# Second wide layer as seven block products for eight, with its down projection a phase behind

## The reference

```python
up = causal_depthwise_conv_2(x @ w_up[l], conv_ffn[l])      # w_up: 1024 x 5632, 3 taps in time
a_ff, b_ff = jnp.split(up, 2, axis=-1)                      # 2816 gate and 2816 value columns
x = layer_norm_2(DEEPNORM_ALPHA * x + (jax.nn.silu(a_ff) * b_ff) @ w_down[l], ln2_g[l], ln2_b[l])
```

## Time and profile before

| what | value |
|---|---|
| median of 3 runs | 3225.45 us (3222.04 to 3225.76) |
| profiled execution, its own time | 3221.95 us |
| span of the profiled execution | 3220.2 us |
| mean granted TensorE clock | 0.962 of full |
| second wide layer, first up product to end | 2453.5 to 3220.2 us |
| PE busy in the whole span | 2994.7 us (93%) |

### The profile page before, as it was taken

The page is one execution under the profiler, slowest core; times in us unless marked ns, Lnnn a source line. Parts: engine busy times, 40 slices in busy tenths (PEclk is TensorE's granted clock), DMA queues, the critical chain, the costliest instruction groups (busy, mean ns, idle before and its releaser), DMA issues.

```text
span 3220.2 us, 35921 instructions
## 1 busy us (share of the span) xinstructions
PE 2994.7 (93%) x15137; PEld 2466.7 (77%) x15137; DVE 1542.0 (48%) x2205; ACT 915.1 (28%) x1250; POOL 784.2 (24%) x482
## 2 busy tenths in 40 slices
PE   8979976689999999999999899799999999999997
PEld 7767766567788788888878899666677888888885
DVE  4775657756644365565244344211135333343335
ACT  3211255422443311112265122211112223222231
POOL 0343401013233322123121454101212211121113
PEclk9989987789999999999999999899999999999999
DMA  4121231122333532212011100211121111111112
GB/s 141 55 60 62 71 97 56 60 98 79 105 113 110 191 114 88 105 66 97 19 53 40 47 21 14 80 58 33 40 92 40 53 40 53 40 52 53 40 53 78
DMA packets 183360, 222.40 MB, mean 69 GB/s; under 512 B 8528, under 2 KB 146448, under 8 KB 181152
## 3 DMA queue, kind: packets, MB, share of 16 engines
q1 hardware_dynamic: 174528, 208.46, 20.0%
q10 hardware_dynamic: 8672, 11.65, 1.0%
HBM read 179.02 MB, written 41.07 MB: 68 GB/s over the span
## 4 chain that ended last, share of the span: by engine, by line
PE 79%; DVE 11%; POOL 3%; ACT 3%; DMA 2%; issue 2%; SPq 0%; ACTq 0%; POOLq 0%; DVEq 0%
PE bank L127 77%; DVE f L158 5%; POOL f L158 3%; DVE f L166 2%; PE bank L142 2%; DVE f L175 1%; DVE r L158 1%; ACT f L147 1%; ACT f L150 1%; DMA f<-gr_s 1%; ACT r L150 1%; DVE f L163 1%; DMA f<-x 0%; DMA f<-w_in 0%; SPq L195 0%
## 5 line engine op out<-in xcount | busy, mean ns | idle before, releaser
L127 PE MATMUL bank<-r,r 128*128 128x512 f32 (+5 forms) x11412 | 2404.0, 372 | 42.6 <-DVE r L158 21.1
L127 PEld LDWEIGHTS bank<-r,r 128*128 128x128 f32 (+1 forms) x11412 | 1984.3, 190 | 452.9 <-issue 44.9
L158 POOL TENSOR_TENSOR f<-f 128x512 f32<-128x512 f32 (+5 forms) x249 | 363.1, 1465 | 1365.1 <-DVE f L166 445.0
L158 DVE TENSOR_TENSOR f<-f,bank 128x512 f32<-128x512 f32 (+2 forms) x564 | 349.6, 641 | 581.1 <-PE bank L127 506.4
L150 ACT ACTIVATE r<-f 128x2048 fp32r<-128x2048 f32 (+4 forms) x188 | 298.7, 1616 | 610.0 <-DMA f<-a_s 248.9
L150 ACT ACTIVATE f<-bank 128x512 f32<-128x512 f32 (+5 forms) x393 | 202.0, 520 | 663.8 <-PE bank L127 600.3
L158 POOL TENSOR_TENSOR r<-f,r 128x2048 fp32r<-128x2048 f32 (+1 forms) x48 | 220.3, 4590 | 623.0 <-ACT r L150 623.0
L127 PE MATMUL bank<-f 128*128 128x128 f32 (+8 forms) x2296 | 326.2, 308 | 43.1 <-ACT f L150 14.4
L158 DVE TENSOR_TENSOR r<-f,r 128x2048 fp32r<-128x2048 f32 (+4 forms) x140 | 258.9, 1860 | 208.1 <-ACT r L150 206.5
L166 DVE SCALAR_TENSOR_TENSOR f<-f,f 128x1024 f32<-128x1024 f32 (+3 forms) x167 | 194.9, 1175 | 306.5 <-ACT f L147 277.4
L127 PEld LDWEIGHTS bank<-f 128*128 128x128 f32 (+2 forms) x2296 | 280.3, 204 | 75.0 <-issue 19.3
(11 more groups left out here) (32 smaller groups left out, 553.4 us busy)
## 6 DMA issues: line engine op xcount, KB each, us to landing
f<-w_in SPq DMA_DIRECT2D x31, 1024.0 KB, 5.5
f<-w_up SPq DMA_DIRECT2D x44, 512.0 KB, 5.1
f<-w_mlp_in SPq DMA_DIRECT2D x64, 256.0 KB, 3.2
a_s<-f SPq DMA_DIRECT2D x64, 256.0 KB, 2.1
f<-w_mlp_out SPq DMA_DIRECT2D x16, 1024.0 KB, 4.9
f<-a_s SPq DMA_DIRECT2D x16, 1024.0 KB, 7.0
f<-w_down SPq DMA_DIRECT2D x11, 1024.0 KB, 4.9
f<-w_out SPq DMA_DIRECT2D x8, 1024.0 KB, 5.2
```

Source lines behind the costliest of these rows:

```text
L127: return self.g.matmul(out, lhs, rhs, start=start, stop=stop, skip_group_check=True)
L158: return self.g.tensor_tensor(out, a, b, op)
```

## The change

The second wide layer gets the scheme of the first. Block 0 is still made by four full products (`U.first`). Blocks 1 to 21 are each made by P1 to P7. ACT's prefix copies and DVE's additions write straight into `raw`. The taps of a block's gate tile (`tap(n, 0)`) come at the end of its turn, those of its value tile (`tap(n - 1, 1)`) in the next turn, after the first addition. The product of gate and value (POOL) goes to DRAM, H is moved out to DRAM and back, and the down projection runs after all blocks, as in the first wide layer. The code of the first layer moves into shared classes without a change of its order. The core of the difference:

```diff
 def pe_f(k, g):
-    for j in range(22):
-        for n, (e, h) in enumerate(S.order(j)):
...
-            g.sum3(b, [((vs[0][:, x, :], vs[1][:, x, :]), (xh[:, x, hs], xl[:, x, hs])) for x in range(8)]).then_inc(
-                *k.up("up products", "f", "up", j, e, h))
-        if j % 2 and 1 < j < 21:
-            i = j // 2 - 1
-            pe_down(k, g, "f", [(i, S.down[i])], S.panels, S.acts)
-    pe_down(k, g, "f", [(i, S.down[i]) for i in (9, 10)], S.panels, S.acts, 4)
+    for n, (e, h) in enumerate(S.order()):
+        if n == 2:
+            pe_flush(k, g, "o2", k.g.H)
+        U.first(g, S.first, "o2", e, h)
+    U.begin(g, 1)
+    for n in range(1, 22):
+        x = k.bank("f", "x", n)
+        U.side(g, n, "z", [2, 3], 2, True)
+        y = U.side(g, n, "y", [4, 5], 5, False)
+        g.wait_ge(*k.past("f", "s1", n))
+        U.product(g, n, 6, x, False, False)
+        g.wait_ge(*k.past("f", "s5", n))
+        U.product(g, n, 3, y, False, True)
+        g.wait_ge(*k.past("f", "s2", n))
+        U.product(g, n, 7, x, False, False)
+        if n < 21:
+            U.begin(g, n + 1)
+        g.wait_ge(*k.past("f", "c22", n))
+        U.product(g, n, 4, x, False, True)
+    D.products(g)
+    for c in range(NC):
+        D.last_products(g, c)

 def act_f(k, g):
+    for n in range(1, 22):
+        if n > 1:
+            c21(n - 1)
+        tap(n - 1, 1)
+        if n < 21:
+            U.round(g, n + 1, 0)
+        else:
+            D.round(g, 0, "d")
+        prefix("s5", n, 1, 1, 5, "y")
+        if n < 21:
+            U.round(g, n + 1, 1)
+        else:
+            D.round(g, 0, "a")
+        prefix("s2", n, 0, 1, 6, "x")
+        tap(n, 0)
+        if n < 21:
+            prefix("s1", n + 1, 0, 0, 1, "x")
+        if n == 1:
+            silu(0)
+        silu(n)

 def dve_f(k, g):
+    U.low_t(g, S.t2, S.kept)
+    taps(0, 0)
+    for n in range(1, 22):
+        add(n, 0, 0, "s1", 2, "z").then_inc(*k.drain("relu low", "f", "z", n))
+        taps(n - 1, 1)
+        if n < 21:
+            U.sums(g, n + 1)
+            U.rest(g, n + 1, 0)
+        else:
+            D.weight_low(g, 0)
+        add(n, 0, 1, "s2", 3, "y").then_inc(*k.drain("relu low", "f", "y", n))
+        if n < 21:
+            U.rest(g, n + 1, 1)
+        add(n, 1, 1, "s5", 7, "x").then_inc(*k.up("relu low", "f", "c22", n))
+        taps(n, 0)

 def pool_f(k, g):
+    U.t4(g, "o2", S.kept, S.t2)
+    for n in range(22):
+        g.wait_ge(*k.past("f", "silu", n))
+        g.wait_ge(*k.past("f", "tap", n, 1, 0))
+        g.tt(S.acc[n % 2], S.acc[n % 2], S.gate, MUL).then_inc(*k.up("squares", "f", "gated", n))
+        if n == 20:
+            D.acts_low(g, 0)

 def sp_f(k, g):
+    sp_away(k, g, "f", "o2", H, 0)
...
+    for n in range(1, 22):
...
+            g.wait_ge(*k.past("f", "P", n - 1, 4))
+            if n < 21:
+                U.load(g, n + 1, "A22")
+            else:
+                down(0)
+        g.wait_ge(*k.past("f", "P", n, 5))
+        if n + 2 < 22:
+            U.load(g, n + 2, "A11", "A12", "A21")
...
+        store(n - 1)
```

More of the change, by code:

```diff
@@ L2148, in pe_flush, with operand_rows @@
         pe_turn(k, g, tag, H[:, c, :], c)
[L2153 to L2206, removed]
+def operand_rows(k, hi, lo):
+    return tuple(v[:, at:at + 2048].rearrange("p (k t) -> p k t", k=4) for v, at in ((k.rb, hi), (k.rb, lo), (k.sb, lo)))
 class Seven:
@@ L2444, in sp_m @@
             g.wait_ge(*k.past("m", "P", 15, 6))
[L2445 to L2448, removed]
+            sp_back(k, g, "m", H)
         store(n, 1)
@@ L2468, in pe_m @@
 def pe_m(k, g):
-    S, U = k.m, k.m.seven
+    S, U, D = k.m, k.m.seven, k.m.down
     a_done(k, g)
@@ L2760, in dve_m @@
             U.rest(g, n + 1, 1)
[L2762 to L2780 removed]
+    D.adds(g, k.H)
     for c in range(NC):
@@ L2783, in dve_m @@
             S.gating.rest(g, 0, 0)
-        add(15, 13, c)
-        g.wait_ge(*k.past("drain", "m", "down", 15, c, 1))
+        D.last_adds(g, k.H, c)
         dve_ln(k, g, "m", c, k.H[:, c, :])
@@ L3804, in o2_done, with order, made @@
+        self.gate = k.sb[:, Y + 7168:Y + 7168 + NT]
+        self.lnw = k.sb[:, Y:Y + 2048]
+        homes = [((ring, X), (ring + 2048, X + 2048)), ((M, M + 2048), (M + 4096, M + 6144)), ((W, W + 2048), (W + 4096, W + 6144))]
+        self.down = Down(k, "f", k.A["w_down_2"], homes, 11)
+    def order(self):
+        return [(e, h) for h in range(2) for e in range(2)]
+    def made(self, n, e, h):
+        return ("drain", "f", "first", e, h) if n == 0 else ("f", f"c{e + 1}{h + 1}", n)
 def o2_done(k, g):
@@ L3879, in act_f, with tap @@
-    S.panels.round(g, S.down[10] + 1)
+    def tap(n, e):
+        for h in range(2):
+            g.wait_ge(*k.past(*S.made(n, e, h)))
+        if e:
+            if n:
+                g.wait_ge(*k.past("f", "gated", n - 1))
+        elif n >= 2:
+            g.wait_ge(*k.past("f", "stored", n - 2))
+        cw = P["conv_ffn"][:, 3 * (n + 22 * e):3 * (n + 22 * e) + 3]
+        o = S.gate if e else S.acc[n % 2]
+        g.act(o, S.raw[n % 2][e][:, 2:2 + NT], ACT.Identity, scale=cw[:, 2:3]).then_inc(*k.up("relu", "f", "tap", n, e, 2))
@@ new lines, in silu, with first @@
+    def silu(n):
+        o = S.acc[n % 2]
+        g.wait_ge(*k.past("f", "tap", n, 0, 0))
+        g.act(o, o, ACT.Silu).then_inc(*k.up("relu", "f", "silu", n))
+    def first(u):
+        e, h = S.order()[u]
+        g.wait_ge(*k.past("f", "first", e, h))
+        g.cp(S.raw[0][e][:, half_slice(h, 2)], k.bank("f", "first", e, h)).then_inc(*k.drain("relu", "f", "first", e, h))
+    first(0)
+    first(1)
+    act_block(k, g, U, "o2", S.kept, 6)
+    act_block(k, g, U, "o2", S.kept, 7)
+    U.high_t1(g, "o2")
@@ new lines, in act_f, with copy, prefix, c21 @@
+    U.round(g, 1, 0)
+    first(2)
+    U.high_t2(g, S.t2)
+    U.round(g, 1, 1)
+    first(3)
+    tap(0, 0)
+    U.high_t34(g)
+    def copy(name, n, e, h, p, bank):
+        if n >= 2:
+            g.wait_ge(*k.past("f", "tap", n - 2, e, 0))
+        g.wait_ge(*k.past("f", "P", n, p))
+        return g.cp(S.raw[n % 2][e][:, half_slice(h, 2)], k.bank("f", bank, n))
+    def prefix(name, n, e, h, p, bank):
+        copy(name, n, e, h, p, bank).then_inc(*k.up("relu", "f", name, n))
+    def c21(n):
+        copy("c21", n, 1, 0, 4, "x").then_inc(*k.drain("relu", "f", "x", n))
+        k.also("f", "c21", n)
@@ L3908, in dve_f, with taps, add @@
-    S.panels.rest(g, S.down[10] + 1, 0)
-    dve_down(k, g, "f", 10, k.g.H, 8, lambda c: dve_ln(k, g, "f", c, k.g.H[:, c, :], S.lnw))
+    def taps(n, e):
+        cw = P["conv_ffn"][:, 3 * (n + 22 * e):3 * (n + 22 * e) + 3]
+        o = S.gate if e else S.acc[n % 2]
+        for d in (1, 0):
+            g.wait_ge(*k.past("f", "tap", n, e, d + 1))
+            g.stt(o, S.raw[n % 2][e][:, d:d + NT], cw[:, d:d + 1], o, MUL, ADD).then_inc(*k.up("relu low", "f", "tap", n, e, d))
+    def add(n, e, h, s, p, bank):
+        o = S.raw[n % 2][e][:, half_slice(h, 2)]
+        g.wait_ge(*k.past("f", s, n))
+        g.wait_ge(*k.past("f", "P", n, p))
+        return g.tt(o, o, k.bank("f", bank, n), ADD)
@@ L3912, in pool_f @@
+    taps(21, 1)
+    D.adds(g, k.g.H)
+    for c in range(NC):
+        D.last_adds(g, k.g.H, c)
+        dve_ln(k, g, "f", c, k.g.H[:, c, :], S.lnw)
 def pool_f(k, g):
-    S = k.f
+    S, U, D = k.f, k.f.seven, k.f.down
     o2_done(k, g)
```

576 lines of the change are left out of this document (290 added, 286 removed).

## The result

The changed kernel takes 3253.43 us (median of 4 runs, 3249.55 to 3254.47) against 3223.74 us of the kernel before on the same chip (4 runs, 3219.76 to 3225.76): ratio 1.0091, 95% interval 1.0074 to 1.0109. It is slower by some 29.7 us. The time is in the prediction's whole range (3210 to 3262), but outside the range of its likeliest case (3224 to 3250), which had 3236. The course is that of the rival "a fall behind every wait", which gave 3257. (A fall is a stretch at the lower of TensorE's two clock levels.)

What follows compares the result with a forecast made beforehand. PE was taken to bound the second layer: 66.9 us saved, waits of 2.80 per block eating 53.2; with all legs, entry and tail +1.1, plus +10 for clock falls, giving 3236 us on the median, range 3210 to 3262.

Steps and rivals of the forecast that it cites:

- likeliest case: Whole kernel: PE waits 2.80 us per block and a third of the waits bring a clock fall; 3236 us, chance 0.47.
- a fall behind every wait: Rival, second layer's turns: each wait before P7 is followed by the lower clock, +1 + 30, 3257 us, chance 0.13.
- The saving: Second wide layer on PE: 288 matmuls fewer ahead of 3167.64, worth 66.9 us at 232.2 ns each.
- The start: Second layer, from the start to block 1's P7: 54.2 us, including 1.6 for a lower clock.
- The wait in each turn: Before P7, blocks 2 to 20: path 10.86 against 8.06, so PE waits 2.80 us, released by ACT's copy s2.
- the bare four: DVE's four weight sums with no POOL instruction among them: 2.42 us.
- The third rival: POOL does not get between DVE's sums: they take 2.4, PE waits 0.4 per block; 3181 us, chance 0.14.
- The turn, the down projection and its drain: After block 20: last turn and transition 28.5, nine down pairs 200.6, then 24 matmuls and drain 5.8 us.
- Entry and end: Before the second layer's first product +1.0 us from extra copies; at the tail +1.5 us from chunk 1's later products.
- I take a third: Clock falls behind the 19 waits: between none and all (30 us), a third assumed, +10 us.
- clock 0.5 shows up in most turns: Sign that the forecast is wrong: the lower clock level in most turns; none would also count against it.
- lower bound of 3210: Low end of the whole range 3210 to 3262, given as 3227 less twice its error, leaving out the third rival.

Runs made afterwards that it cites:

- the filled kernel: Changed kernel plus eight matmuls that nobody reads ahead of TensorE's wait on s2 in each of 20 turns: 3222.87 us, ratio 1.0.
- the first experiment: Changed kernel with VectorE's four sums of the next block put before the value taps: 3166.49 us, ratio 0.9825.
- The second experiment: Changed kernel with taps still ahead of the sums, but POOL's gating product waiting for the sums to end: 3183.0 us, ratio 0.9882.
- the fourth: Changed kernel with the value taps moved even earlier, ahead of the addition for c11: 3205.13 us, ratio 0.9942.
- the fifth: Changed kernel plus a second, unread POOL product of 128x512 ahead of the gating product in 19 blocks: 3282.97 us, ratio 1.0176.
- the kernel with the eighth product back: Changed kernel in the order of the first experiment, plus 12 unread matmuls in each of 21 turns ahead of the wait on c22: 3218.34 us, ratio 0.9984.

## Why the prediction came out as it did

- **The saving**, 66.9 us at 232.2 ns a matmul: right. Where nothing waits the pace holds over 1560 matmuls (231.3 ns each) and over 1908 (232.3). The 131 ns of the Trainium skill ("TensorE: Matmul & The Clock Gate", Back-to-back issue gap) does not hold for this kernel's matmuls; no stretch came near it.
- **The start**, 54.2: measured 53.2 (2450.61 to 2503.78).
- **The wait in each turn**: right in place, cause and releaser. The path is 10.98 (10.86 predicted). A turn without a fall is 22.5, not 22.30, so the wait in issue is 3.0, not 2.80: 0.12 more path and 0.08 less work of PE beside it. That is +3.8 over 19 turns, and it reads as 2.77 to 2.87 idle, not 2.5 to 2.6. Inside the sums two terms were off and nearly cancel: the bare four take 2.74, not 2.42, and POOL's product adds 2.21, not 2.40. Both parts of the wait are shown: with POOL's product out of the sums 0.56 to 0.66 is left of it, with the taps out as well nothing, and a POOL product of 1.04 more adds 1.0. The Trainium skill ("SBUF — State Buffer", SBUF: two separate sides) states an exclusive lock on the shared ports for a whole instruction. The trace agrees: the sums grow by nearly the product's length.
- **The third rival**, sums of 2.4: out, they take 4.95.
- **The turn, the down projection and its drain**, 28.5 + 200.6 + 5.8 = 234.9: measured 233.5 (2961.69 to 3195.18).
- **Entry and end**: +1.0 and +1.5 predicted. The end is 52.5 for 52.6 before, so 0. The first product stands at 2450.61 for 2453.48; the later kernels, with nothing changed ahead of it, have it anywhere from 2450.49 to 2456.84, so the 2.9 is scatter of the stages before, and the layer alone is the better measure: 797.1 from its first product to the end, 766.7 before, +30.4.
- **The clock: the step that failed.** "I take a third": +10. Measured: a fall in every turn, 24.10 less 22.5 = 1.6 a turn, 30.4 over the 19, and 30.6 by the filled kernel. The price of one fall (1.6) was right, the share wrong, and the prediction itself names "clock 0.5 shows up in most turns" as a sign of being wrong. I placed an idle time of 2.55 between 2.15 without a fall and 3.33 with one, and weighed by distance, as if the length of a wait alone decided. It does not, and the place counts. The 2.15 stood in the last turn of the first layer. In that place the twelve traces have eight waits of 2.05 to 2.66 without a fall and four of 2.94 to 3.04 with one, while in the repeated turns 16 of 18 waits of 2.08 to 2.19 had one. So the 2.15 said little about a wait in a repeated turn.

PE's timelines in the last turn of the first layer, first the kernel after, then the first experiment (24 matmuls at full clock take 5.8):

```profile
1103.30 7.36 PE L127 MATMUL bank<-r,r 128*128 128x512 f32 x24 [2.94 <-ACT f L150]
```

```profile
1105.67 5.80 PE L127 MATMUL bank<-r,r 128*128 128x512 f32 x24 [2.66 <-ACT f L150]
```

The same holds for the last turn of the second layer: the wait of 2.90 at 2982.84 in the first timeline above has 24 matmuls in 5.77 behind it, so no fall, though it is longer than each of the 18 waits of 2.76 to 2.87 that have one. The second experiment has 3.00 there and the fourth 2.96, without a fall, the fifth 2.99 and the kernel with the eighth product back 2.41, with one.

In sum for the 19 turns: 457.9 measured, 423.7 predicted ahead of the clock, 34.2 = 30.4 of clock + 3.8 of wait. The rest of the legs came 2.4 lower.

That the rival's 3257 came so near is in part luck. Its sum for the profiled execution is +31, and +27.5 was measured: 3.8 more of wait stand against 2.4 less in the other legs, 1.5 less at the end and 3.9 less at the entry, which is mostly scatter. The range's lower bound of 3210 does not follow from its working either (3227 less twice 6 is 3215); nothing hangs on it.

The Trainium skill ("TensorE: Matmul & The Clock Gate", Why this matters for your kernels) advises to keep idle gaps of TensorE under about 3 us. By it the waits of 2.8 would still have been safe, 3227 in my sum. In the repeated turns the runs show falls behind most waits from 1.86 us on; there the measurement decides. Single waits of 2.66 to 3.00 without a fall would agree with the page.

What stays open: what beside its length decides whether a wait between 1.86 and 3.00 us has a fall behind it. In the twelve traces, of the waits of 1.3 us and more ahead of 128x512 matmuls of rounded operands, from the first wide layer to the end, none below 1.86 has one and none above 3.00 is without; between them there are both, in the repeated turns mostly with, in the last turns mostly without. Open is also why every second fall lasts longer at 3.74.

## What to carry to other kernels

A product saved on TensorE counts in full only while no chain over the other engines sets the turn, so lay out the turn's longest chain first and put everything with later readers behind it: moving one call turned 0.9% slower into 1.8% faster. On that chain, a GpSimd instruction that runs beside VectorE instructions with both inputs in SBUF adds nearly its own length (2.21 us for a product of 2.40, 0.99 for one of 1.04). And a short wait that repeats is worth more than it seems when the clock falls behind it: here 2.8 us of waiting cost another 1.6 us each time, and a wait under about 1.7 us, reached by a shorter path or by five or eight spare matmuls in it, removed that part. Three or four spare matmuls did not.

## What was not expected of the hardware

- In the repeated turns the passage is narrow: idle 1.63 to 1.73, no fall in 18 turns; 1.86 to 1.95, 16 of 18. One matmul of 0.23 us per turn decides over some 27 us (one execution of each kernel). Yet single waits of 2.90, 2.96 and 3.00 in the last turn have none.
- 160 matmuls without a reader made the kernel 30.6 us faster.
- A fall costs the same 1.6 us behind 1.9 us of idle time as behind 2.85, and up to 1.0 more in every second turn behind 3.74.
- POOL's product grows too when it meets VectorE's sums: 2.72 beside them, 2.40 in the first experiment's place.
